# Two feature blocks of the first modulation summed along the row by VectorE instead of by TensorE

## What is computed

```python
mod = jax.nn.silu(c) @ w_mod[l] + b_mod[l]          # condition of the latent tokens
mod_c = jax.nn.silu(c_ctx) @ w_mod[l] + b_mod[l]    # condition of the context tokens
sh1, sc1, ga1, sh2, sc2, ga2 = jnp.split(mod[:, None, :], N_MOD, axis=-1)
csh1, csc1, cga1, csh2, csc2, cga2 = jnp.split(mod_c, N_MOD)
pc = modulate(rmsnorm(ctx, g_norm_mix[l]), csh1, csc1) @ w_in[l]
p = modulate(rmsnorm(x, g_norm_mix[l]), sh1, sc1) @ w_in[l]
```

## Time and profile before

| | us |
|---|---|
| median of 3 runs | 1866.18 (1864.85 to 1866.75) |
| the profiled execution | 1864.87 |
| its span | 1863.2 |
| TensorE busy | 1593.6 (86%) |
| VectorE busy | 1050.5 (56%) |
| ScalarE busy | 397.9 (21%) |
| GpSimd busy | 438.0 (24%) |
| DMA | 724.64 MB, mean 389 GB/s |

### The profile page before, as it was taken

How to read it: one execution, slowest core, us unless ns; L and a number is a source line. 1 busy time by engine, 2 the same in 40 slices (tenths; PEclk the granted TensorE clock), 3 DMA queues, 4 the chain that set the end, 5 groups by cost and what they waited for, 6 DMA issues and landing times. The chain is left out here.

```text
span 1863.2 us, 13323 instructions
## 1 busy us (share of the span) xinstructions
PE 1593.6 (86%) x4518; PEld 761.0 (41%) x4518; DVE 1050.5 (56%) x1706; ACT 397.9 (21%) x1168; POOL 438.0 (24%) x384
## 2 busy tenths in 40 slices
PE   6999999999999979999877886877759687687776
PEld 2355445565458854443333332333324233232332
DVE  2237775675558873433546556465665656646445
ACT  2121013222010023222212222221223212122112
POOL 0000000001005565556322222221213122121212
PEclk9999999999999989999999999999889898999999
DMA  9998866548978999999999999999999999999997
GB/s 401 427 376 351 336 256 247 214 186 348 421 276 346 418 422 422 421 421 421 425 428 427 428 428 427 428 428 428 428 427 415 428 429 428 428 427 428 428 428 303
DMA packets 73442, 724.64 MB, mean 389 GB/s; under 512 B 7432, under 2 KB 9816, under 8 KB 20000
## 3 DMA queue, kind: packets, MB, share of 16 engines
q0 software_dynamic: 53472, 613.75, 78.8%
q1 hardware_dynamic: 17264, 107.30, 14.1%
q10 hardware_dynamic: 2640, 2.75, 0.5%
HBM read 721.63 MB, written 2.15 MB: 388 GB/s over the span
## 5 line engine op out<-in xcount | busy, mean ns | idle before, releaser
L1318 PE MATMUL ps<-ring,wg 128*128 128x512 f32 x1168 | 541.0, 613 | 130.5 <-ACT wg L851 111.0
L1766 DVE SCALAR_TENSOR_TENSOR ring<-ring,A 128x2048 f32<-128x2048 f32 x142 | 324.6, 2291 | 307.3 <-DMA ring<-in_expert_rows,acc 223.1
L1318 PEld LDWEIGHTS ps<-ring,wg 128*128 128x128 f32 x1168 | 221.8, 195 | 444.6 <-issue 275.8
L1023 PE MATMUL ps<-ring,H 128*128 128x512 f32 x512 | 222.1, 593 | 2.2 <-ACT rows_and_values L655 2.1
L513 POOL DMA_INDIRECT ring<-in_expert_rows,acc x106 | 116.1, 1095 | 388.7 <-PE ps L1318 376.5
L846 ACT ACTIVATE rows_and_values<-rows_and_values 128x1 f32<-128x1 f32 x256 | 50.9, 199 | 704.6 <-DVE ring L1766 398.4
L1318 PE MATMUL ps<-H,wg 128*128 128x512 f32 x360 | 167.3, 612 | 30.1 <-ACT wg L851 29.4
L1345 DVE SCALAR_TENSOR_TENSOR ring<-ring,rows_and_values 128x2048 f32<-128x2048 f32 x64 | 143.7, 2287 | 49.2 <-DMA ring<-in_mod_late 36.2
L1318 PE MATMUL ps<-rows_and_values,wg 128*128 128x512 f32 x288 | 135.5, 614 | 36.6 <-ACT wg L851 35.9
L1023 PEld LDWEIGHTS ps<-ring,H 128*128 128x128 f32 x512 | 96.4, 190 | 122.0 <-issue 118.9
L851 ACT ACTIVATE wg<-K,rows_and_values 128x128 f32<-128x128 f32 x256 | 102.7, 401 | 161.3 <-PE ps L1318 154.7
(11 more groups left out here) (281 smaller groups left out, 1464.4 us busy)
## 6 DMA issues: line engine op xcount, KB each, us to landing
ring<-in_mod_late POOLq DMA_DIRECT2D x32, 2048.0 KB, 10.5
ring<-in_mod_first SPq DMA_DIRECT2D x16, 2048.0 KB, 20.6
ring<-in_w_in SPq DMA_DIRECT2D x14, 2048.0 KB, 11.4
ring<-in_w_query SPq DMA_DIRECT2D x7, 2048.0 KB, 14.6
ring<-in_w_out SPq DMA_DIRECT2D x12, 1024.0 KB, 10.1
H<-in_tokens SPq DMA_DIRECT2D x4, 1024.0 KB, 13.0
queries_and_gates<-in_w_in SPq DMA_DIRECT2D x2, 1024.0 KB, 23.9
queries_and_gates<-neg_rows ACTq DMA_DIRECT2D x8, 256.0 KB, 5.2
```

Of the source, the lines that this page charges most:

```text
L1023: ins = mm(bank, H[:, kk, b * P:(b + 1) * P], W[kh][:, k, :], **flags)
L1318: ins = mm(ps[:, 4 * b + n, :], diag[:, r % 4, :], row[:, n * CH:(n + 1) * CH], start=k == 0, stop=r == BLOCK_RANKS - 1, skip_group_check= ...
L1766: v.scalar_tensor_tensor(out=rows_u, in0=rows_u, scalar=1.0, in1=A[:, r // BLOCK_RANKS, :], op0=ALU.mult, op1=ALU.mult, accum_out=dots[:, ...
```

## The change

The last step (feature blocks 14 and 15) is taken out of the chain on TensorE. `PE_STEPS` is 7: TensorE computes blocks 0 to 13, with pieces 0 to 13. The weights of blocks 14 and 15 arrive turned, as two tiles of 2 MB, one per block, which hold its shift and its scale rows. They are loaded into A and B. Four scalar_tensor_tensor instructions per tile sum it along the row, for shift and scale and for both conditions (`sum_turned`), each waiting for the one ahead. This needs the context condition as a row too: GpSimd loads it right behind the other condition, both now at `w_free` 6, and ScalarE applies its silu to the two rows behind blocks 5 and 7 instead of at the end.

```diff
 STEPS, STEP_K = 8, KB // 8
+PE_STEPS = 7
+TURNED = KB - PE_STEPS * STEP_K
...
+            def load_turned(i):
+                sp.wait_ge(S["squares_psum"], 1)
+                sp.dma_start((A, B)[i][:], mod_turned[i]).then_inc(S[f"ld_turned{i}"], 16)
...
                 load_early(q)
+                if q == 3:
+                    load_turned(1)
+                    continue
                 load_moda(4 * q + 2)
+                if q == 2:
+                    load_turned(0)
                 load_moda(4 * q + 3)
...
-            pool.wait_ge(S["w_free"], 8)
+            pool.wait_ge(S["w_free"], 6)
             pool.dma_start(condition_row, condition.to_broadcast([P, D])).then_inc(S["ld_condition"], 16)
+            pool.dma_start(context_row, context_condition.to_broadcast([P, D])).then_inc(S["ld_condition"], 16)
...
             pool.wait_ge(S["w_free"], 16)
+            pool.wait_ge(S["mod_ready"], STEPS)
             nc.gpsimd.memset(acc[:, 3, :], 0.0).then_inc(S["row_zero"], 1)
...
+                if k in (5, 7):
+                    row = (condition_row, context_row)[k // 2 - 2]
+                    act.wait_ge(S["ld_condition"], 32)
+                    nc_a.activation(row, row, ACT.Silu).then_inc(S["condition_ready"], 1)
...
-                if k >= KB - 2:
+                if k >= KB - 2 - TURNED:
                     ins.then_inc(S["w_free"], 1)
...
-            for step in range(1, STEPS):
-                more = step + 1 < STEPS
+            for step in range(1, PE_STEPS):
+                more = step + 1 < PE_STEPS
...
+            for k in range(KB - TURNED, KB):
+                project_early(k)
...
+            def sum_turned(i):
+
+                k = KB - TURNED + i
+                dve.wait_ge(S[f"ld_turned{i}"], 16)
+                dve.wait_ge(S["condition_ready"], 2)
+                for a, to in ((0, shT), (1, gT)):
+                    tile = (A, B)[i][:, a, :]
+                    for c_, row in ((0, condition_row), (1, context_row)):
+                        link(v.scalar_tensor_tensor(
+                            out=products if c_ == 0 else tile, in0=tile, scalar=1.0, in1=row, op0=ALU.mult,
+                            op1=ALU.mult, accum_out=to[:, c_, k:k + 1]))
+
             for step in range(STEPS):
-                collect_mod(step)
+                if step < PE_STEPS:
+                    collect_mod(step)
                 modulation(step)
                 for k in range(STEP_K * step, STEP_K * (step + 1)):
                     scale_tokens(k)
+                if step in (4, 5):
+                    sum_turned(step - 4)
```

More of the change, by code:

```diff
@@ L175, in laid_out @@
         "x": x, "tokens": np.ascontiguousarray(tokens), "vectors": np.ascontiguousarray(vectors), "gate_bias": gate_bias,
-        "mod_first": np.ascontiguousarray(first.transpose(4, 0, 2, 1, 3, 5)).reshape(STEPS, 2, P, KH * CH),
+        "mod_first": np.ascontiguousarray(first.transpose(4, 0, 2, 1, 3, 5)[:PE_STEPS]).reshape(PE_STEPS, 2, P, KH * CH),
+        "mod_turned": np.ascontiguousarray(w_mod[0][:, :2 * D].T.reshape(2, KB, P, D)[:, KB - TURNED:].transpose(1, 2, 0, 3)),
+        "context_condition": c_ctx.reshape(1, D),
         "mod_late": np.ascontiguousarray(w_mod[0][:, 2 * D:].T.reshape(MODB, 2, 2, P, D).transpose(0, 1, 3, 2, 4)
@@ L187, in laid_out, with build @@
     }
-def build(nc, x, tokens, vectors, gate_bias, mod_first, mod_late, condition, w_in, w_gates, w_out, w_query,
+def build(nc, x, tokens, vectors, gate_bias, mod_first, mod_turned, context_condition, mod_late, condition, w_in, w_gates, w_out, w_query,
           keys, g_norm_ffn, g_fourier, g_mlstm, g_final, expert_u, expert_v, expert_rows, consts, out):
@@ L251, in build @@
         add4 = K[:, C_SEL:C_SEL + 2]
-        vecz = flat(acc)[:, CH:2 * CH].rearrange("p (k j) -> p k j", k=KB)
+        vecz = VXf[:, 3 * CH:4 * CH].rearrange("p (k j) -> p k j", k=KB)
         gate_sel = K[:, C_GATE:C_GATE + NG]
@@ L275, in build @@
         h2T = yT
-        condition_row = modrow
+        condition_row, context_row = modrow, flat(acc)
+        products = VXf[:, D:2 * D]
         new_rows = acc[0:KB, 0, :]
@@ L311, in build @@
         mod_dram = nc.dram_tensor("mod_rows", (4, D), F32, kind="Internal").ap()
-        names = """ym_ready first_picked picked top_ready pick_step ld_const ld_dft ld_vec ld_h0 ld_h1 ld_h2 ld_h3 sq_act sq_dve squares_psum squares_ready mean_psum std_ready rstd_ready scaled ht ld_wg ld_bg ld_gy
-        ld_x2 ld_gffn st_mod ld_ga1 ld_sc2 ld_sh2 rows_psum rows_spread ld_keys ld_wq2 ld_gfin row_zero ld_condition condition_ready row_cols ld_ga2 silu_c vecz_zero vecz_ready moda_free
+        names = """ym_ready first_picked picked top_ready pick_step ld_const ld_dft ld_vec ld_h0 ld_h1 ld_h2 ld_h3 sq_act sq_dve squares_psum squares_ready mean_psum std_ready rstd_ready scaled ht ld_gates ld_gy
+        ld_x2 st_mod ld_ga1 ld_gain2 ld_sh2 rows_psum rows_spread ld_keys ld_wq2 ld_gfin row_zero ld_condition ld_turned0 ld_turned1 condition_ready row_cols ld_ga2 silu_c vecz_zero vecz_ready moda_free
         modcol_psum mod_ready std w_free m_free row_sum
@@ L445, in _ @@
         def _(pool):
-            pool.wait_ge(S["w_free"], 8)
+            pool.wait_ge(S["w_free"], 6)
             pool.dma_start(condition_row, condition.to_broadcast([P, D])).then_inc(S["ld_condition"], 16)
+            pool.dma_start(context_row, context_condition.to_broadcast([P, D])).then_inc(S["ld_condition"], 16)
             pool.wait_ge(S["w_free"], 14)
-            pool.dma_start(wg[:], w_gates.rearrange("p (k n) -> p k n", k=KB)).then_inc(S["ld_wg"], 16)
-            pool.dma_start(bg[:], gate_bias).then_inc(S["ld_bg"], 16)
+            pool.dma_start(wg[:], w_gates.rearrange("p (k n) -> p k n", k=KB)).then_inc(S["ld_gates"], 16)
+            pool.dma_start(bg[:], gate_bias).then_inc(S["ld_gates"], 16)
             pool.wait_ge(S["w_free"], 16)
+            pool.wait_ge(S["mod_ready"], STEPS)
             nc.gpsimd.memset(acc[:, 3, :], 0.0).then_inc(S["row_zero"], 1)
@@ L495, in _ @@
             pool.dma_start(B[:, 1, :], x[0, P:2 * P, :]).then_inc(S["ld_x2"], 16)
-            pool.dma_start(g2, g_norm_ffn.to_broadcast([P, D])).then_inc(S["ld_gffn"], 16)
+            pool.dma_start(g2, g_norm_ffn.to_broadcast([P, D])).then_inc(S["ld_gain2"], 16)
             pool.wait_ge(S["row_free"], 3)
-            spread(2, sc2, "ld_sc2")
+            spread(2, sc2, "ld_gain2")
             load_from(MODB_LATE + 1, MODB)
@@ L982, in _ @@
                 project_early(STEP_K * step + 1)
+            for k in range(KB - TURNED, KB):
+                project_early(k)
             def gate_parts_of_projection():
-                pe.wait_ge(S["ld_wg"], 16)
+                pe.wait_ge(S["ld_gates"], 32)
                 for k in range(KB):
@@ L1378, in modulation @@
                 both = lambda t: t.unsqueeze(1).to_broadcast([P, 2, STEP_K])
[L1379 to L1382, removed]
+                if step < PE_STEPS:
+                    dve.wait_ge(S["modcol_psum"], step + 1)
+                    cols = ps[:, 7, 0:4 * KB].rearrange("p (a k c) -> p a c k", a=2, c=2)
+                    sums = cols[:, 0, :, ks], cols[:, 1, :, ks]
+                else:
+                    sums = shT[:, :, ks], gT[:, :, ks]
+                v.tensor_tensor(shT[:, :, ks], sums[0], both(bias[:, 0, ks]), ALU.add)
+                link(v.tensor_tensor(gT[:, :, ks], sums[1], both(bias[:, 1, ks]), ALU.add))
                 v.scalar_tensor_tensor(out=gT[:, :, ks], in0=gT[:, :, ks], scalar=1.0,
@@ L1472, in scans @@
                                 ).then_inc(S["thr_in"], 1)
-            dve.wait_ge(S["condition_ready"], 1)
             def conv_q(j):
@@ L1648, in _ @@
                 if n == 0:
-                    dve.wait_ge(S["ld_gffn"], 16)
-                    dve.wait_ge(S["ld_sc2"], 16)
+                    dve.wait_ge(S["ld_gain2"], 32)
                     v.scalar_tensor_tensor(out=g2, in0=sc2, scalar=1.0, in1=g2, op0=ALU.add,
```

4 lines of the change are left out of this document (1 added, 3 removed).

## The result

| | us |
|---|---|
| before, median of 6 runs | 1865.76 (1864.85 to 1866.75) |
| changed, median of 6 runs | 1882.39 (1881.90 to 1882.88) |
| ratio | 1.009, 95% interval 1.008 to 1.010 |
| changed, profiled execution | 1882.09, span 1880.3 |

The change costs 16.6 us. The forecast was 1882.9 us, 1874 to 1889.

The account below looks back on a forecast made before the run. DMA transfers were taken to bound the first stage. Tile landing 109.4 + sums 9.5 + copy 0.7 + signals 0.1 + tail 18.4 + clock 2.7 = 140.8 us, 16.7 later; 1866.2 + 16.7 = 1882.9 us, range 1874 to 1889.

Parts of the forecast that it names:

- What bounds: From 20 to 124 us the DMA engines lead and TensorE runs just behind; later stages pass a delay through.
- the 4.5 us of idle time: TensorE's idle time from 124 to 560 us, which could absorb at most 4.5 us of the delay.
- First turned tile: Ahead of piece 11: tile lands at 86.9, piece 11 at 91.8; sums just covered before step 5's columns at 97.2.
- ScalarE: One more silu from 60 to 124 us costs nothing; rows land well before blocks 6 and 8 need ScalarE.
- Second turned tile: Lands last, 109.4 us; sums 9.5 us delay step 6's copy to 119.7; TensorE waits some 11 us at its columns.
- Removed work: On TensorE, step 7's two partial products, 3.57 us, and its columns, 0.81 us: 4.4 us saved.
- The tail of 18.4 us: TensorE from step 6's columns to the gate projection: 22.8 us before, less the 4.4 removed.
- rival 3: Sums wholly beside TensorE's work in the first stage, so its 4.4 us come off: 1861.8 us; chance 0.03.
- The clock: TensorE's stop at step 6's columns lowers its granted clock behind it: 2.7 us lost, bounds 0 to 4.5.
- Rival 1: Second turned tile lands out of turn, near 101 us; gate matmul 5.6 us late, 1871.8 us; chance 0.12.
- Rival 2: Late modulation, starting 24 us later, makes VectorE's lateness replace TensorE's: 20 to 25 us, 1886 to 1891 us; chance 0.07.

Follow-up runs that it names:

- e2: Changed kernel without the transfer of the context condition's row, which VectorE fills with ones instead: 1879.26 us.
- e7: Changed kernel with the second turned tile loaded behind piece 11, ahead of pieces 12 and 13: 1872.14 us, ratio 1.0036.
- e9: Kernel before with the last early weight tile loaded behind piece 15 and the latent condition's row asked for at count 16 instead of 8: 1863.41 us, ratio 0.9988.
- e4: Kernel before with 2 instead of 16 partial matmuls in step 7, all transfers and columns kept: 1865.15 us, ratio 0.9997.
- e1: Changed kernel with the second turned tile's four sums behind the scaling of step 6 instead of ahead of its copy: 1875.64 us, ratio 1.0053.
- e3: Changed kernel with only two of the four sums of the second turned tile: 1877.50 us.
- e5: Changed kernel with GpSimd's late modulation beginning at the 18th instead of the 16th count of w_free: 1884.60 us.
- e6: Changed kernel with 8 more matmuls, whose result nobody reads, between block 10 and the columns of step 6: 1879.22 us.
- e10: e8 with 3 more matmuls, whose result nobody reads, between the two partial products of step 6: 1867.40 us, ratio 1.0009.
- e8: Changed kernel with turned tiles loaded behind pieces 11 and 13, sums behind step 5, step 6 and block 14: 1868.18 us, ratio 1.0013.

## Why the prediction was right

**What bounds.** Right. The transfers lead the first stage (e2, e7, e9; e4, where less TensorE work changed next to nothing), and the shift at the gate projection went through to the end: 16.6 us there, 16.6 in the medians. None of the 4.5 us of idle time absorbed any.

**First turned tile.** Right. Tile at 86.9 forecast, 86.75 measured; piece 11 at 91.8, measured 91.67. I had not reckoned with the clock behind this stop of 5.4 us (the partial product took 3.64 us at a granted clock of 0.50, 1.2 GHz), which took the columns of step 5 to 98.9 instead of 97.2. It cost nothing, since the second tile came later still; it only made the stop ahead of the columns of step 6 shorter, 8.2 us where I had forecast some 11.

**ScalarE.** Right in effect, too sure in wording. The context row landed only at 70.8 us, 19.8 us after its issue, and ScalarE waited 11.96 us for it with block 6 behind. TensorE wanted that block at 76.4; ScalarE finished its modulation at about 73.5. The "well before" was a margin of 3 us.

**Second turned tile.** Right, term by term: landing 109.4, measured 108.77; four sums 9.5, measured 9.33 (108.77 to 118.10); columns at 119.7, measured 118.85. e1 confirms the place, e3 the sums' length, e2 and e7 what the landing depends on.

**Removed work.** The tail of 18.4 us held: in e7, at full clock, the same stretch takes 18.2 us (111.55 to 129.71). But the prediction booked all 4.4 us as gained and then let the late tile take them back. e4 shows that with nothing added the partial products were worth 0.9 us. This does not touch the sum, which runs from the tile's landing; it touches rival 3, whose full 4.4 us e4 does not bear out.

**The clock.** Mis-sized: 2.7 us taken, 3.5 measured (118.85 to 140.76 is 21.9 us, less 18.4; 3.8 against e7's 18.2), within the bounds of 0 to 4.5. The 0.8 us by which it was short and the 0.8 us by which the columns came early (tile 0.6, sums 0.2) cancelled. That the gate projection stands at 140.76 for a forecast of 140.8 is luck in this last part; the terms are good to about 1 us.

**Rival 1**, the tile out of its turn, did not occur. What the Trainium skill says in DMA: Bandwidth & Descriptors, section Queues, rings and completion order, that completion is not first-in-first-out per issuing engine, may hold in general. Here the transfers on SyncE's queue that the argument needs landed in the order of issue: A at 86.75, piece 11 at 91.67, B at 108.77 and the constants, 32.6 us after their issue at 77.8, at 110.4 us, A and B within 0.6 us of the forecast from the bytes ahead. Between queues the order did not hold: GpSimd's context row, issued at 51.0, landed by 70.8 us, ahead of piece 9, which was issued by 50.3 and waited for until 74.5. **Rival 2**, the late modulation, did not occur either. GpSimd's first late piece went out at 134.5 us and the first late row sum started at 142.56, as forecast. The prediction named only the spare before the scans, 8.42 us, and overlooked the earlier meeting at the first turned row (e5). There the spare was 10.2 us, of which the change took 2.8 (10.2 to 7.4).

## What to carry to other kernels

Where the DMA engines are full, a piece of work is priced by the bytes that stand ahead of its last input and by what is left to do behind it, not by the engine time that it frees; moving work to an idle engine gains nothing if its input is last in the queue. In an engine's fixed order, put a wait for the latest transfer behind everything that is ready sooner: here that alone was 7 of 17 us. And look in a full queue for bytes that are asked for before they are needed, which was the only gain found here.

## What the hardware showed beyond that

The granted clock can fall behind a stop of about 2 us in one profiled execution and hold in another. All kernels have an idle of 2.08 us on TensorE, some 145 us behind the gate projection, where it waits for a copy by ScalarE. This is the 32-matmul stretch behind it in the changed kernel, in e6 and in e9, each time with the same idle:

```profile
285.25 13.97 PE L1043 MATMUL ps<-ring,H 128*128 128x512 f32 x32 [2.08 <-ACT rows_and_values L673]
```

```profile
283.71 15.67 PE L1046 MATMUL ps<-ring,H 128*128 128x512 f32 x32 [2.08 <-ACT rows_and_values L673]
```

```profile
266.65 15.67 PE L1024 MATMUL ps<-ring,H 128*128 128x512 f32 x32 [2.08 <-ACT rows_and_values L656]
```

In the first the clock stays at 1.00; in e6 it reads 0.66 over the following 5 us, and 1.7 us are gone. The kernel before, e1, e5 and e10 show the first form, e2, e3, e4, e7 and e8 the second: the clock fell in 7 of 12 profiled executions. What decides it was not found. It may be part of the scatter of 2 to 3 us between executions, and it accounts for 1.7 of the 2.0 us that e9's profiled execution (span 1863.2 us, as the kernel before) gained at the gate projection and had lost again by the end. An experiment that moves TensorE by 2 us is therefore to be read from the stretch that it changes as well as from the total.
